# A three-layer block on one core: six tiles change places in SBUF

## The chip, the cores and the metric

The kernel runs on one core of one Trainium2 chip, in one launch. The metric is the device time of one execution in microseconds (us). The kernel before took 1033.55 us as the median of three runs (1032.76, 1033.91 and 1033.55).

## The reference, cut to what matters

The input is one sequence of 256 tokens with 1024 features, in fp32. It goes through two layers of a first block and then one layer of a second block:

```
for i in range(2):                                    # first block
    h = rmsnorm(x, norm1_g[i])
    mix = hybrid_mixer(h, w_in[i], ...)               # three kinds of attention, 16 heads of 64
    x = x + mix @ w_out[i]
    h = rmsnorm(x, norm2_g[i])
    a, u = split(h @ w_up[i], 2)                      # 2 x 2816 columns
    x = x + (silu(causal_conv(a) + conv_b[i]) * u) @ w_down[i]
h = rmsnorm(x, final_g)
u = rms_norm(h, norm_mix_pre)                         # second block
proj = u @ w_in                                       # ten slots of 256, and gates 4 x 1024
ys = [rg_lru, pool, hgrn2, short_conv](proj)          # four branches of 256 columns
merged = sum_k sigmoid(gate_k) * (ys[k] @ w_branch[k])
h = h + rms_norm(merged @ w_out, norm_mix_post)
hid = square(relu(rms_norm(h, norm_mlp_pre) @ w_up))  # 4096 columns
h = h + rms_norm(hid @ w_down, norm_mlp_post)
```

Nearly all of the arithmetic is in the products with the weight matrices.

## The kernel before, in words

**Weights and their split.** The weights come in pieces of 128 x 2048 fp32 (1 MB) through a ring of four buffers, the tile `raw`. A weight is used as the sum of two fp32r numbers, a high and a low part: ScalarE writes the high part `whi` (L1288), VectorE (L1744) or GpSimd (L2575) the difference `wlo`. Both have three slots. The activations are split in the same way, so a product of an activation and a weight is three matmuls: high by high, high by low, low by high.

**The activations' tiles.** `hb2` holds the normed input of a layer, 8 feature tiles with the high and the low part side by side (`hh` and `hl`). The names `gh` and `gl` hold the high and the low part of what goes into a second product: the hidden units of the feed-forward parts (written at L1421 and L2105, and at L1718 and L2540), part of the attention's output, and the branches of the second block. `mg` holds one quarter of the second block's merged sum. `mskt` holds the attention masks and an identity in bf16. `prmt` holds small parameters and an fp32 identity. `PQ` is a large working area; `E`, `rl`, `PT`, `gb`, `sm`, `sc`, `cc` and `th` are smaller ones.

**Which role each tile has on TensorE.** A matmul has a stationary operand, which a weight load brings into the array ahead of it, and a moving one, which streams through. In the up projections (L697, L702, L703) `whi` and `wlo` are stationary and `hb2` moves. In the down projections (L720 to L722, and L734 to L736), the branch products (L1211 to L1213) and part of the output products (L577, L578, L580) a 128 x 128 piece of `gh`, `gl` or `mg` is stationary and 512 columns of `whi` or `wlo` move. In the transposes (L554 of `X`, L773 of `PQ`, L926 of `E` and `XN`) the tile that is turned is stationary and the identity in `prmt` moves. In the profile's names the moving tile stands first, the stationary one second.

**Order.** The program of each engine is written out by hand, and the engines meet by semaphores alone. Feed-forward stage j has TensorE make 256 hidden units (16 matmuls with 512 columns and 16 with 256), ScalarE and VectorE evict, convolve and gate them, and TensorE take the 24 matmuls of a down projection a stage later. All loads are issued by the sync engine's queue; `mskt` is loaded once, near the start (L2658), and first read by L1860.

**Where tiles lie.** No address is written in the kernel. Each `sb(...)` call asks for the next piece of every SBUF partition, in the order in which the calls stand (L162 to L186). The built program begins this list at byte 16512 of a partition and rounds each start up to a multiple of 32 bytes.

Of the kernel before, what the change touches and what calls it, by code (L numbers as in the profile page):

```python
# [8 lines left out]
F32R = mybir.dt.float32r  # L9
BF16 = mybir.dt.bfloat16  # L10
# [5 lines left out]
L = 256  # L16
# [128 lines left out]
def program(nc, wst, prm, msk, prm2, gains, lvl, x, out):  # L145
    ctx = ExitStack()
    with ctx:
        def sb(name, shape, dt=F32):
            return ctx.enter_context(nc.sbuf_tensor(name, shape, dt))
# [12 lines left out]
        wlo = sb("wlo", [128, SPL, CH], F32R)  # L162
        X = sb("X", [128, 2, D])
        XN = sb("XN", [128, 2, D])
        mskt = sb("mskt", [128, 9, 128], BF16)
        hb2 = sb("hb2", [128, 8, 2, L], F32R)
        hh, hl = hb2[:, :, 0, :], hb2[:, :, 1, :]
        gh = sb("gh", [128, 2, 2, L], F32R)
        gl = sb("gl", [128, 2, 2, L], F32R)
        mg = sb("mg", [128, 2, 2, L], F32R)  # L170
        prmt = sb("prmt", [128, NPRM])
        PQ = sb("PQ", [128, 2 * PCOLS + 22 * L])
        P = PQ[:, 0:2 * PCOLS].rearrange("p (t c) -> p t c", t=2)
        QT = PQ[:, 2 * PCOLS:].rearrange("p (j q) -> p j q", q=L)
        gb = sb("gb", [128, D])
# [4 lines left out]
        sc = sb("sc", [128, 2, L])  # L180
        selm = sb("selm", [128, 2, L], BF16)
        vbd = sb("vbd", [80, 5, 64])
        cc = sb("cc", [128, 2, L])
        th = sb("th", [128, 2, L])
        lv = sb("lv", [128, 8, 128], mybir.dt.uint16)
# [6 lines left out]
        def par2(name):  # L192
            a, w = at2[name]
            return PQ[:, a:a + w]

# [14 lines left out]
        def space(n):  # L210
            a = spare["pq"]
            spare["pq"] += n
            assert spare["pq"] <= 2 * PCOLS + 22 * L
            return PQ[:, a:a + n]

# [2415 lines left out]
        def sync_program(e):  # L2631
# [24 lines left out]
            for m in range(2, NT):  # L2656
# [4 lines left out]
                if m == second:  # L2661
                    q.wait_ge(*x_new[("out", 1), 1, 1])
                    e.dma_start(PQ[:, 0:NPRM2], prm2).then_inc(s_prm2, 16)
                    e.dma_start(lv[:, :, :], lvl).then_inc(s_lvl, 16)
# [186 lines left out]
```

## Time and profile before

| | |
|---|---|
| median of three runs | 1033.55 us |
| the profiled execution's own time | 1032.76 us |
| its span, first to last instruction | 1031.5 us |
| TensorE matmuls busy | 1021.1 us, 99% of the span, 5714 matmuls |
| TensorE weight loads busy | 857.8 us, 83% |
| VectorE busy | 765.6 us, 74% |
| ScalarE busy | 551.6 us, 53% |
| GpSimd busy | 224.8 us, 22% |
| DMA | 179.16 MB, 174 GB/s over the span |

"Busy" of TensorE is the time in which at least one matmul is under way. Matmuls overlap: one with 512 columns has a duration of about 0.39 us, while the next one starts 0.23 us after it. What sets the pace of a row of matmuls is therefore the distance between starts, not the duration. A weight load stands in a row of its own (PEld), and it runs beside the matmul before it.

### The profile page before, as it was taken

The numbers are of one execution on the slowest core, as the hardware profiler recorded it, in microseconds if no ns is written. First come the engines' busy times: TensorE is split into PE (matmuls) and PEld (weight loads), VectorE is DVE, ScalarE is ACT, GpSimd is POOL, SyncE is SP. The second block draws the span as 40 slices with busy tenths as digits, with TensorE's granted clock in tenths as the row PEclk, the third lists the DMA queues.
The fourth block names the chain that finished last, engine by engine and source line by source line (L and its number), as shares of the span: only waits on it lengthen the run. The fifth ranks groups of instructions, "written<-read, shape, count | busy, mean of one in ns | idle before, by whom it ended". The sixth has DMA issues, their size and how long they took to land.

```text
span 1031.5 us, 14779 instructions
## 1 busy us (share of the span) xinstructions
PE 1021.1 (99%) x5714; PEld 857.8 (83%) x5714; DVE 765.6 (74%) x1221; ACT 551.6 (53%) x831; POOL 224.8 (22%) x311
## 2 busy tenths in 40 slices
PE   8999999999999999999999999999999999999997
PEld 6877788888888877788888888998888878888886
DVE  6987678788777887578787778978855457666665
ACT  6575656555456466656455556755434545434432
POOL 0270600000000280600000003128967620000000
PEclk9999999999999999999999999999999999999999
DMA  9451445555554351365554554543535555455541
GB/s 361 151 203 44 149 178 186 187 191 202 194 184 176 112 213 42 123 223 191 204 204 167 200 186 163 175 172 105 180 124 194 214 184 221 177 207 191 178 149 41
DMA packets 26822, 179.16 MB, mean 174 GB/s; under 512 B 2944, under 2 KB 3072, under 8 KB 6272
## 3 DMA queue, kind: packets, MB, share of 16 engines
q1 hardware_dynamic: 26752, 178.22, 48.6%
q8 instruction: 45, 0.74, 0.3%
q14 instruction: 25, 0.20, 0.1%
HBM read 177.16 MB, written 1.05 MB: 173 GB/s over the span
## 4 chain that ended last, share of the span: by engine, by line
PE 98%; DMA 1%; DVE 1%; ACT 0%; SPq 0%; issue 0%; DVEq 0%
PE pb L697 17%; PE pb L702 10%; PE pb L577 9%; PE pb L578 9%; PE pb L580 8%; PE pb L720 6%; PE pb L722 6%; PE pb L721 6%; PE pb L703 2%; PE pb L958 2%; PE pb L914 2%; PE pb L623 1%; PE pb L622 1%; PE pb L624 1%; PE pb L1124 1%; PE pb L926 1%
## 5 line engine op out<-in xcount | busy, mean ns | idle before, releaser
L1744 DVE TENSOR_TENSOR wlo<-raw,whi 128x2048 fp32r<-128x2048 f32 x127 | 290.6, 2290 | 108.3 <-ACT whi L1288 108.0
L1288 ACT ACTIVATE whi<-raw 128x2048 fp32r<-128x2048 f32 (+1 forms) x164 | 304.9, 1863 | 62.9 <-PE pb L580 31.4
L2575 POOL TENSOR_TENSOR wlo<-raw,whi 128x256 fp32r<-128x256 f32 x260 | 197.6, 798 | 322.8 <-ACT whi L1288 322.6
L697 PE MATMUL pb<-hb,whi 128*128 128x512 f32 x770 | 194.0, 391 | 0.0
L697 PEld LDWEIGHTS pb<-hb,whi 128*128 128x128 f32 x770 | 144.9, 188 | 28.8
L577 PE MATMUL pb<-whi,hb 128*128 128x512 f32 x344 | 137.9, 401 | 0.0
L578 PE MATMUL pb<-wlo,hb 128*128 128x512 f32 x344 | 134.1, 390 | 0.0
L580 PE MATMUL pb<-whi,hb 128*128 128x512 f32 x328 | 128.0, 390 | 0.0
L702 PEld LDWEIGHTS pb<-hb,wlo 128*128 128x128 f32 x880 | 120.0, 190 | 8.6
L702 PE MATMUL pb<-hb,wlo 128*128 128x256 f32 x880 | 122.7, 282 | 0.0
L720 PE MATMUL pb<-whi,gh 128*128 128x512 f32 x280 | 109.3, 391 | 0.0
L722 PE MATMUL pb<-whi,gl 128*128 128x512 f32 x280 | 109.1, 390 | 0.0
L721 PE MATMUL pb<-wlo,gh 128*128 128x512 f32 x280 | 108.9, 389 | 0.0
L2584 POOL TENSOR_TENSOR sm<-sm 128x1 f32<-128x1 f32 x12 | 6.5, 553 | 422.7 <-DVE sm L1752 242.5
L577 PEld LDWEIGHTS pb<-whi,hb 128*128 128x128 f32 x344 | 64.6, 188 | 17.8 <-issue 5.0
L578 PEld LDWEIGHTS pb<-wlo,hb 128*128 128x128 f32 x344 | 64.6, 188 | 12.5
L580 PEld LDWEIGHTS pb<-whi,hb 128*128 128x128 f32 x328 | 61.6, 188 | 13.3
L722 PEld LDWEIGHTS pb<-whi,gl 128*128 128x128 f32 x280 | 52.6, 188 | 11.4
L721 PEld LDWEIGHTS pb<-wlo,gh 128*128 128x128 f32 x280 | 52.6, 188 | 11.1
L720 PEld LDWEIGHTS pb<-whi,gh 128*128 128x128 f32 x280 | 52.7, 188 | 9.6
L1421 ACT ACTIVATE gh<-th 128x512 fp32r<-128x512 f32 x22 | 13.9, 632 | 76.3 <-DVE th L2102 76.3
L703 PE MATMUL pb<-hb,whi 128*128 128x512 f32 x110 | 43.6, 396 | 0.0
(388 smaller groups left out, 1559.2 us busy)
## 6 DMA issues: line engine op xcount, KB each, us to landing
raw<-wst SPq DMA_DIRECT2D x160, 1024.0 KB, 4.8
raw<-wst SPq DMA_DIRECT2D x8, 512.0 KB, 3.6
gb<-gains SPq DMA_DIRECT2D x3, 512.0 KB, 5.6
X<-x SPq DMA_DIRECT2D x2, 512.0 KB, 5.5
out<-X SPq DMA_DIRECT2D x4, 256.0 KB, 2.1
PQ<-prm SPq DMA_DIRECT2D x1, 909.0 KB, 4.7
raw<-wst SPq DMA_DIRECT2D x2, 256.0 KB, 7.5
prmt<-prm SPq DMA_DIRECT2D x1, 479.0 KB, 10.2
```

What stands on the lines that cost most here:

```text
L577: e.matmul(o, high[:, s], wh[:, k, :], start=first and k == 0, stop=False)
L578: mm = e.matmul(o, high[:, s], wl[:, k, :], start=False, stop=False)
L580: mm = e.matmul(o, low[:, s], wh[:, k, :], start=False, stop=last and k == 3)
L697: e.matmul(both, wh[:, k, s], hb2[:, k, :, :].rearrange("p i q -> p (i q)"), start=k == 0, stop=False)
L702: e.matmul(high, wl[:, k, s], hh[:, k, :], start=False, stop=False)
L703: mm = e.matmul(both, wh[:, 7, s], hb2[:, 7, :, :].rearrange("p i q -> p (i q)"), start=False, stop=True)
L720: e.matmul(o, ah, wh[:, k, c], start=j == 0 and k == 0, stop=False)
L721: e.matmul(o, ah, wl[:, k, c], start=False, stop=False)
L722: mm = e.matmul(o, al, wh[:, k, c], start=False, stop=last and k == 1)
L1288: e.activation(whi[:, split_slot(m), 0:w], raw[:, m % RAW, 0:w], ACT.Copy).then_inc(*hi(m))
L1744: e.tensor_tensor(wlo[:, split_slot(m), 0:w], raw[:, m % RAW, 0:w], whi[:, split_slot(m), 0:w].bitcast(F32), ALU.subtract).then_inc(*lo_v(m))
L2575: g = e.tensor_tensor(wlo[:, split_slot(m), s], raw[:, m % RAW, s], whi[:, split_slot(m), s].bitcast(F32), ALU.subtract)
```

## The change

The order of the `sb(...)` calls is changed. No shape, type, instruction, semaphore or loop is touched, and each engine has the same instructions in the same order.

```
         XN = sb("XN", [128, 2, D])
-        mskt = sb("mskt", [128, 9, 128], BF16)
         hb2 = sb("hb2", [128, 8, 2, L], F32R)
         hh, hl = hb2[:, :, 0, :], hb2[:, :, 1, :]
-        gh = sb("gh", [128, 2, 2, L], F32R)
-        gl = sb("gl", [128, 2, 2, L], F32R)
-        mg = sb("mg", [128, 2, 2, L], F32R)
         prmt = sb("prmt", [128, NPRM])
+        mskt = sb("mskt", [128, 9, 128], BF16)
         PQ = sb("PQ", [128, 2 * PCOLS + 22 * L])
...
         vbd = sb("vbd", [80, 5, 64])
+        gh = sb("gh", [128, 2, 2, L], F32R)
+        gl = sb("gl", [128, 2, 2, L], F32R)
+        mg = sb("mg", [128, 2, 2, L], F32R)
         cc = sb("cc", [128, 2, L])
```

What this does to the first byte of each tile within a partition, in the two built programs:

| tile | bytes | start before | start after | moved by | start modulo 64, before and after |
|---|---|---|---|---|---|
| raw, whi, wlo, X, XN | 98304 together | 16512 (raw) | 16512 | 0 | 0, 0 |
| mskt | 2304 | 114816 | 135584 | +20768 | 0, **32** |
| hb2 | 16384 | 117120 | 114816 | -2304 | 0, 0 |
| gh | 4096 | 133504 | 210848 | +77344 | 0, **32** |
| gl | 4096 | 137600 | 214944 | +77344 | 0, **32** |
| mg | 4096 | 141696 | 219040 | +77344 | 0, **32** |
| prmt | 4376 | 145792 | 131200 | -14592 | 0, 0 |
| PQ | 43520 | 150176 | 137888 | -12288 | 32, 32 |
| gb, rl, E, PT, sm, sc, selm, vbd | 29440 together | 193696 (gb) | 181408 | -12288 each | 32, 32 |
| cc, th, lv | 6144 together | 223136 (cc) | 223136 | 0 | 32, 32 |

## Rows read from the trace of the kernel before

**Rows 1.** The page: span, TensorE's busy time, granted clock in 40 slices.
```profile
span 1031.5 us, 14779 instructions
...
PE 1021.1 (99%) x5714; PEld 857.8 (83%) x5714; DVE 765.6 (74%) x1221; ACT 551.6 (53%) x831; POOL 224.8 (22%) x311
...
PEclk9999999999999999999999999999999999999999
```

**Rows 2.** The page: engines' shares of the chain that ended last.
```profile
PE 98%; DMA 1%; DVE 1%; ACT 0%; SPq 0%; issue 0%; DVEq 0%
```

**Rows 3.** Waits of TensorE, longest first: total us, times, longest us.
```profile
PE pb L599 <- ACT whi L1350: 1.8, 1, 1.8
PE pb L541 <- DVE sm L2556: 1.5, 1, 1.5
PE pb L681 <- DVE hb L1766: 0.8, 1, 0.8
```

**Rows 4.** Instructions grouped by line and shape: busy us, mean ns, idle before.
```profile
L720 PE MATMUL pb<-whi,gh 128*128 128x512 f32 x280 | 109.3, 391 | 0.0
...
L577 PE MATMUL pb<-whi,gh 128*128 128x512 f32 x40 | 16.6, 415 | 0.0
...
L1211 PE MATMUL pb<-whi,gh 128*128 128x512 f32 x32 | 13.2, 413 | 0.0
...
L734 PE MATMUL pb<-whi,gh 128*128 128x512 f32 x24 | 9.5, 397 | 0.0
...
L577 PE MATMUL pb<-whi,mg 128*128 128x512 f32 x8 | 3.1, 389 | 0.0
```

**Rows 5.** Timeline of TensorE in a down projection: start us, length us.
```profile
162.18 0.39 PE L722 MATMUL pb<-whi,gl 128*128 128x512 f32 x1
162.41 0.39 PE L720 MATMUL pb<-whi,gh 128*128 128x512 f32 x1
162.63 0.39 PE L721 MATMUL pb<-wlo,gh 128*128 128x512 f32 x1
```

**Rows 6.** Timeline of TensorE in an up projection.
```profile
148.51 1.75 PE L697 MATMUL pb<-hb,whi 128*128 128x512 f32 x7
150.10 1.11 PE L702 MATMUL pb<-hb,wlo 128*128 128x256 f32 x8
151.05 0.40 PE L703 MATMUL pb<-hb,whi 128*128 128x512 f32 x1
151.29 1.77 PE L697 MATMUL pb<-hb,whi 128*128 128x512 f32 x7
152.90 1.12 PE L702 MATMUL pb<-hb,wlo 128*128 128x256 f32 x8
```

**Rows 7.** Weight loads by line: ns min/median/max, first and last start.
```profile
L697 PEld LDWEIGHTS pb<-hb,whi x770: 187/188/192, 148.3 to 1013.4; 128*128 128x128 f32 x193
...
L554 PEld LDWEIGHTS pb<-prmt,X x96: 138/140/143, 4.8 to 848.3; 128*128 128x128 f32 x96
...
L773 PEld LDWEIGHTS pb<-prmt,PQ x84: 97/140/146, 26.3 to 409.3; 128*128 128x128 f32 x76, 128*32 128x32 f32 x4, 128*64 128x64 f32 x4
...
L1124 PEld LDWEIGHTS pb<-PQ,rl x32: 187/188/193, 699.4 to 752.2; 128*128 128x128 f32 x32
```

**Rows 8.** Writers of gh and gl (timeline), and a like group on other tiles.
```profile
154.64 0.63 ACT L1421 ACTIVATE gh<-th 128x512 fp32r<-128x512 f32 x1 [2.15 <-DVE th L2102]
...
155.30 0.69 DVE L2105 TENSOR_TENSOR gl<-th,gh 128x512 fp32r<-128x512 f32 x1 [0.70 <-ACT gh L1421]
...
L2083 DVE TENSOR_TENSOR E<-E,rl 128x512 f32<-128x512 f32 x22 | 15.2, 693 | 0.7
```

**Rows 9.** DMA issues (KB, median us to landing), and mskt's first reader.
```profile
gb<-gains SPq DMA_DIRECT2D x3, 512.0 KB, 5.6
...
mskt<-msk SPq DMA_DIRECT2D x1, 288.0 KB, 14.3
...
L1860 DVE TENSOR_TENSOR sc<-sc,mskt x4: 291/292/294, 40.4 to 360.4; 128x128 f32<-128x128 f32 x4
```

## The prediction

> **What bounds the kernel now.** I read the page first: TensorE has a matmul under way in 1021.1 of 1031.5 us, and the granted clock is at its upper level of 2.4 GHz in all forty slices [rows 1]. The chain that ended last is TensorE for 98% [rows 2]. The waits of TensorE come next: the three longest are 1.8, 1.5 and 0.8 us, each met once, and the longest two stand at the very start [rows 3]. So no other engine and no transfer is late anywhere for long; the kernel lasts as long as its row of 5714 matmuls, and the reader should ask of any edit whether it changes the distance between the starts of two matmuls. I read that distance from the timeline. In a down projection matmuls with 512 columns start at 162.18, 162.41 and 162.63, thus 0.225 us apart [rows 5]. In an up projection eight matmuls with 256 columns take from 150.10 to 151.05, thus 0.119 us each, and seven with 512 columns take from 148.51 to 150.10, thus 0.227 us each [rows 6].
>
> **The change part by part.** No instruction is removed, added or moved on any engine; only starts of tiles change. There are three kinds of change, and I give each a cost.
>
> First, tiles that keep their position within 64 bytes: `hb2`, `prmt`, `PQ` and the eight tiles behind it. Everything moves by a multiple of 64 bytes, and `PQ` with those behind it by one common distance, so that their mutual distances stay. The largest user is the up projection, in which `hb2` streams through the array. If the absolute place counted, the eight slices of `hb2`, which lie 2 KB apart, would stream at unlike rates. They take 1.59 us for seven in one place and 1.61 us (151.29 to 152.90) in the next [rows 6], 0.227 and 0.230 us each, over seven different slices. I take 0. The 0.02 us between the two groups, which are the same slices against other weights, is the largest irregularity of such a row. There are 110 such groups (770 matmuls of L697 by 7 [rows 7]), so 110 x 0.02 = 2.2 us is my bound for what place could give or cost here, in either direction.
>
> Second, `gh`, `gl` and `mg`, which go from 0 to 32 modulo 64 and 77344 bytes up. On TensorE they are always stationary. The matmuls that use them are five groups with counts of 280, 40, 32, 24 and 8 for the product high by high [rows 4], and each has two sisters of the same count for the other two products: 3 x 384 = 1152 matmuls. What changes for each is a weight load. Does a load from 32 modulo 64 take longer? The trace has both kinds. `X` starts at 0 modulo 64 and `PQ` at 32, and their loads have the same median of 140 ns. `whi` starts at 0 and `rl` at 32: 188 ns for both, with maxima of 192 and 193 [rows 7]. So the measured difference is 0 ns at the median. And a longer load would be covered. The fastest row of full loads is that of the 256-column matmuls, one every 0.119 us [rows 6], so a load and all that goes with it fits in 0.119 us; the matmuls on `gh` start 0.225 us apart [rows 5]. A load could grow by about 0.1 us before it showed. What hides it is the stream of the matmul before. I take 0. Without that cover, the one extra nanosecond by which the maxima differ would be 1.2 us (1152 x 1 ns), and the whole spread of a load of `rl`, 193 - 187 = 6 ns, would be 6.9 us; a gain could be as large by the same reckoning if the new place were the better one.
>
> The writers of these tiles are the other half. ScalarE writes `gh` in 0.63 us and VectorE `gl` in 0.69 us, of which the latter ends at 155.99 [rows 8]. The down projection of that stage starts at 159.66, right behind four groups of an up projection that began at 148.51 [rows 6] (eight more matmuls of each kind take 2.79 us, 148.51 + 4 x 2.79 = 159.67). So there is 3.7 us of cover for these two instructions. Their price if they changed: VectorE's operation of the same shape with all three operands on tiles at 32 modulo 64 (`E` and `rl`) takes 693 ns, against 0.69 us for the one whose output and one input are at 0 [rows 8]. I take 0 again. If the cover were gone, a change of 10 ns on each of some 40 such pairs would be 0.4 us, for better or worse.
>
> A rule bears on this half. The Trainium skill, page "Vector Engine (DVE) Microarchitecture Reference", section 5.2, says that VectorE streams at full rate only if its runs of words start on an 8-byte boundary, and gives 1.30 against 1.054 ns per column where both sources start on an odd word. Were the new starts odd words, its estimate for 512 columns would be 126 ns more per operation; at a start that is a multiple of 32 the rule sees no change, and the equal 0.69 us of the two kinds of rows [rows 8] agrees.
>
> Third, `mskt`, which also goes to 32 modulo 64. Its transfer of 288 KB lands 14.3 us after its issue, that is at about 20 us, and its first reader starts at 40.4 us [rows 9], so 20 us of cover. Transfers into a tile at 32 modulo 64 are in the trace too (`gb`, 512 KB in 5.6 us), so a multiple of the time is not to be feared; `mskt` waits in a queue of weight transfers, and even if it took twice its share (288 KB at 512 KB in 5.6 us is 3.2 us) nothing on the path would wait for it but the weights behind it. I take 0, with 0 to 3.2 us as bounds if the weights behind it were awaited by TensorE, and as much the other way.
>
> Sum: 0 us on the profiled execution, whose own time is 1032.76 us (1031.5 us of span and 1.3 us around it). That run was the fastest of the three shown; their median is 0.79 us above it. Unchanged work should land at the median, so I predict 1033.5 us.
>
> **The rivals.**
>
> *Slower: the loads of `gh`, `gl` and `mg` become visible.* The mechanism would be a load that has to fetch more from a start at 32 modulo 64, or collides with ScalarE and VectorE, which write `cc` and `th` right behind it in SBUF, and does so in a part that the stream before doesn't cover. With 6 ns on 1152 matmuls it gives 1033.5 + 6.9 = 1040.4 us; it leaves the band of no change from 1.8 ns each on (2.07 / 1152). For it speaks only that the three tiles are the ones whose position within 64 bytes changes, and that they are used 1152 times. Against it speak the equal medians [rows 7] and the room of 0.1 us.
>
> *Faster: the present place costs something.* A matmul with 512 columns would stream in 0.213 us at 2.4 GHz, and starts are 0.225 to 0.227 apart. If a part of those 12 to 14 ns were a collision due to the place of `gh` next to `hb2`, the move could give it back: 4 ns on 1152 matmuls is 4.6 us, thus 1028.9 us. Against it: the up projection, which doesn't touch `gh`, has the same 0.227 [rows 6], so the surplus belongs to every matmul.
>
> A rule speaks against both. The Trainium skill, page "SBUF — State Buffer", section "Who interferes with whom", gives TensorE two read ports of its own, for the moving operand and for the load, and names the port pair of VectorE and GpSimd as the only place of contention; no address enters it. By it alone the change is worth 0. The rows of one pace on all tiles agree, so it strengthens the forecast's chance and changes no number.
>
> *Nothing on TensorE, but the start is disturbed.* If the load of `mskt` held the weights behind it back while TensorE is nearly dry, up to 3.2 us would be added: 1036.7 us. Against it: after 0.8 us at most TensorE waits for nothing there [rows 3].
>
> That the change doesn't do what it says can be left out: the starts in the two built programs are those of the table.
>
> **How the numbers follow.** The forecast of no effect gets 0.88, the slower rival 0.05, the disturbed start 0.02, the faster rival 0.05. What a measurement of this kernel can tell from no change is about 0.2%, 2.07 us, so the band is 1031.5 to 1035.6 us. The chances are then 0.05 for faster, 0.88 for the same and 0.07 for slower. The range holds the forecast's own bounds: below, 2.2 us of irregularity (1031.3); above, the like 2.2 us and a little of the loads (1035.8). The rivals lie outside it with 0.12.
>
> **What would show each step right or wrong.** Right: starts in the down projections still 0.225 to 0.227 us apart, loads of `gh` at 188 ns, L1421 at 0.63 and L2105 at 0.69 us, seven `hb2` matmuls in 1.59 to 1.61 us, the same three waits of TensorE, and the landing of `mskt` far ahead of 40 us. A wider distance at L720 to L722 with L697 unchanged would show the slower rival; a narrower one the faster; later first weights the third. I am wrong if the time leaves 1031.5 to 1035.6 us with the granted clock unchanged.

## The result and the profile after

The changed kernel takes 1039.61 us as the median of four runs (1039.45 to 1042.50), against 1033.73 us for the kernel before beside it: a ratio of 1.0061 with a 95% interval of 1.0046 to 1.0077. It is slower by about 6 us, and outside the range that I gave. Executions of one kernel can differ by some 3 us, and by the traces most of that lies ahead of the first product on `gh` (which starts at 106.0 us in the kernel before and as late as 109.2 us in others), so a median of few runs can lie up to 3 us too high, and the lowest times stand beside the medians below.

The page and the waits of TensorE look as before, with a longer span:

```profile
span 1038.1 us, 14777 instructions
...
PE 1027.8 (99%) x5712; PEld 858.0 (83%) x5714; DVE 766.0 (74%) x1221; ACT 551.6 (53%) x831; POOL 224.5 (22%) x311
...
PEclk9999999999999999999999999999999999999999
...
PE 98%; DMA 1%; DVE 1%; ACT 0%; issue 0%; SPq 0%; DVEq 0%
```

The busy time of TensorE has grown by 6.7 us (1021.1 to 1027.8), the span by 6.6 us [rows 1]; the granted clock is the same. No engine waits in a new place. TensorE's waits after the change (total us, times, longest) are those of [rows 3], to a tenth:

```profile
PE pb L599 <- ACT whi L1350: 1.8, 1, 1.8
PE pb L541 <- DVE sm L2556: 1.5, 1, 1.5
PE pb L681 <- DVE hb L1766: 0.8, 1, 0.8
```

So the matmuls themselves have become slower, and the groups by line and shape tell which (busy us, mean ns of one):

```profile
L697 PE MATMUL pb<-hb,whi 128*128 128x512 f32 x770 | 194.7, 392 | 0.0
L577 PE MATMUL pb<-whi,hb 128*128 128x512 f32 x344 | 137.9, 401 | 0.0
...
L702 PE MATMUL pb<-hb,wlo 128*128 128x256 f32 x880 | 122.7, 282 | 0.0
L722 PE MATMUL pb<-whi,gl 128*128 128x512 f32 x280 | 110.9, 396 | 0.0
L720 PE MATMUL pb<-whi,gh 128*128 128x512 f32 x280 | 110.6, 395 | 0.0
L721 PE MATMUL pb<-wlo,gh 128*128 128x512 f32 x280 | 110.5, 395 | 0.0
...
L577 PE MATMUL pb<-whi,mg 128*128 128x512 f32 x8 | 3.2, 396 | 0.0
```

Before, L720 had 391 ns and L577 with `mg` 389 ns [rows 4]; L721 and L722, which I had not shown, had 389 and 390 ns. The products on `hb2` are unchanged (L577) or nearly so (L697, 0.7 us more over 770). Each product with `gh`, `gl` or `mg` stationary is longer on average, by 4 to 7 ns in most groups and by 2 to 3 ns in the 120 of L577, L578 and L580 on `gh` and `gl`.

The pace is in the timeline. One down projection after the change, its first matmuls and the first of what follows (start us, length us):

```profile
159.88 0.39 PE L720 MATMUL pb<-whi,gh 128*128 128x512 f32 x1
160.11 0.40 PE L721 MATMUL pb<-wlo,gh 128*128 128x512 f32 x1
160.35 0.39 PE L722 MATMUL pb<-whi,gl 128*128 128x512 f32 x1
...
162.21 0.40 PE L721 MATMUL pb<-wlo,gh 128*128 128x512 f32 x1
162.44 0.40 PE L722 MATMUL pb<-whi,gl 128*128 128x512 f32 x1
162.67 0.40 PE L720 MATMUL pb<-whi,gh 128*128 128x512 f32 x1
162.91 0.40 PE L721 MATMUL pb<-wlo,gh 128*128 128x512 f32 x1
...
165.47 0.85 PE L697 MATMUL pb<-hb,whi 128*128 128x512 f32 x3
```

The same stretch in the kernel before:

```profile
159.66 0.39 PE L720 MATMUL pb<-whi,gh 128*128 128x512 f32 x1
...
165.13 1.07 PE L697 MATMUL pb<-hb,whi 128*128 128x512 f32 x4
```

24 matmuls take 5.59 us instead of 5.47, 0.233 us each instead of 0.228. (The 0.225 us that the prediction read from [rows 5] came from three rounded starts.) That is 5 ns per matmul, and from the starts of all of them I count 4.6 us over the 840 of L720 to L722; the other 312 with these tiles give 1.4 us more, and the 770 matmuls of L697 0.7 us. Together this is 6.7 us, which accounts for the 6.6 us of the span.

The loads of these tiles, on which I had built my argument, show nothing at all. After the change (ns min/median/max):

```profile
L720 PEld LDWEIGHTS pb<-whi,gh x280: 186/188/192, 159.7 to 1026.1; 128*128 128x128 f32 x140
...
L722 PEld LDWEIGHTS pb<-whi,gl x280: 187/188/188, 160.1 to 1026.6; 128*128 128x128 f32 x140
```

### The profile page after: what moved, and what is told of

Same layout as the page of the kernel before. It is cut to its first block, busy times and chain, and to the rows that moved or that the text cites. A ratio compares the mean times of both kernels' runs of the same rounds, so it can differ in the third digit from the quotient of the medians.

```text
span 1038.1 us, 14777 instructions
## 1 busy us (share of the span) xinstructions
PE 1027.8 (99%) x5712; PEld 858.0 (83%) x5714; DVE 766.0 (74%) x1221; ACT 551.6 (53%) x831; POOL 224.5 (22%) x311
## 4 chain that ended last, share of the span: by engine, by line
PE 98%; DMA 1%; DVE 1%; ACT 0%; issue 0%; SPq 0%; DVEq 0%
PE pb L697 17%; PE pb L702 10%; PE pb L577 9%; PE pb L578 9%; PE pb L580 8%; PE pb L722 6%; PE pb L721 6%; PE pb L720 6%; PE pb L703 2%; PE pb L958 2%; PE pb L914 2%; PE pb L623 1%; PE pb L624 1%; PE pb L622 1%; PE pb L1124 1%; PE pb L926 1%
## 5 line engine op out<-in xcount | busy, mean ns | idle before, releaser
L697 PE MATMUL pb<-hb,whi 128*128 128x512 f32 x770 | 194.7, 392 | 0.0
L697 PEld LDWEIGHTS pb<-hb,whi 128*128 128x128 f32 x770 | 144.9, 188 | 29.8
L577 PE MATMUL pb<-whi,hb 128*128 128x512 f32 x344 | 137.9, 401 | 0.0
L578 PE MATMUL pb<-wlo,hb 128*128 128x512 f32 x344 | 134.1, 390 | 0.0
L580 PE MATMUL pb<-whi,hb 128*128 128x512 f32 x328 | 128.1, 391 | 0.0
L702 PEld LDWEIGHTS pb<-hb,wlo 128*128 128x128 f32 x880 | 120.1, 190 | 8.7
L702 PE MATMUL pb<-hb,wlo 128*128 128x256 f32 x880 | 122.7, 282 | 0.0
L722 PE MATMUL pb<-whi,gl 128*128 128x512 f32 x280 | 110.9, 396 | 0.0
L720 PE MATMUL pb<-whi,gh 128*128 128x512 f32 x280 | 110.6, 395 | 0.0
L721 PE MATMUL pb<-wlo,gh 128*128 128x512 f32 x280 | 110.5, 395 | 0.0
L577 PEld LDWEIGHTS pb<-whi,hb 128*128 128x128 f32 x344 | 64.6, 188 | 17.9 <-issue 5.0
L578 PEld LDWEIGHTS pb<-wlo,hb 128*128 128x128 f32 x344 | 64.7, 188 | 12.7
L580 PEld LDWEIGHTS pb<-whi,hb 128*128 128x128 f32 x328 | 61.6, 188 | 13.2
L722 PEld LDWEIGHTS pb<-whi,gl 128*128 128x128 f32 x280 | 52.6, 188 | 12.6
L721 PEld LDWEIGHTS pb<-wlo,gh 128*128 128x128 f32 x280 | 52.6, 188 | 12.5
L720 PEld LDWEIGHTS pb<-whi,gh 128*128 128x128 f32 x280 | 52.7, 188 | 11.0
L1421 ACT ACTIVATE gh<-th 128x512 fp32r<-128x512 f32 x22 | 13.9, 632 | 76.3 <-DVE th L2102 76.3
```

Source lines behind the costliest of these rows:

```text
L577: e.matmul(o, high[:, s], wh[:, k, :], start=first and k == 0, stop=False)
L578: mm = e.matmul(o, high[:, s], wl[:, k, :], start=False, stop=False)
L580: mm = e.matmul(o, low[:, s], wh[:, k, :], start=False, stop=last and k == 3)
L697: e.matmul(both, wh[:, k, s], hb2[:, k, :, :].rearrange("p i q -> p (i q)"), start=k == 0, stop=False)
L702: e.matmul(high, wl[:, k, s], hh[:, k, :], start=False, stop=False)
L720: e.matmul(o, ah, wh[:, k, c], start=j == 0 and k == 0, stop=False)
```

## The experiments

Every experiment changes only where tiles lie. `gap` and `gap2` are tiles that nobody uses. Where room was needed, the tile `sm` was cut from 1152 to as few as 1120 columns, which suffice. Since the starts themselves turned out not to be what counts, the table gives differences of starts modulo 256, which is where the series ended; the texts on record speak of 64 and 128, as I thought at the time. The ratio is near that of the means of all executions, not of the medians, and is taken against the kernel before beside each run (whose medians there were 1033.0 to 1033.7 us). The last column is read from the traces: how much longer than in the kernel before the part of the span is that begins with the first product on `gh`. It leaves out the early stretch in which executions of one kernel differ.

| kernel | gh minus whi | hb2 minus whi | median us (lowest) | ratio to before, 95% interval | behind the first use of gh, us |
|---|---|---|---|---|---|
| before | 0 | 0 | 1033.73 (1032.76) | | |
| after | 32 | 0 | 1039.61 (1039.45) | 1.0061 (1.0046 to 1.0077) | +6.5 |
| high place, 64 | 64 | 0 | 1042.32 (1040.32) | 1.0072 (1.0057 to 1.0087) | +6.4 |
| old place, 32 | 32 | 0 | 1043.09 (1040.41) | 1.0072 (1.0054 to 1.0090) | +7.6 |
| hb2 shifted | 64 | 32 | 1045.91 (1045.80) | 1.0110 (1.0093 to 1.0127) | +11.6 |
| weights shifted | 32 | 32 | 1045.04 (1044.89) | 1.0103 (1.0085 to 1.0120) | +10.8 |
| high place, 0 | 0 | 0 | 1033.20 (1032.70) | 1.0005 (0.9992 to 1.0017) | 0.0 |
| all shifted by 32 | 0 | 0 | 1032.77 (1032.62) | 0.9989 (0.9980 to 0.9999) | -0.1 |
| all at multiples of 512 | 0 | 0 | 1035.24 (1032.82) | 1.0010 (1.0000 to 1.0021) | +0.1 |
| gh at 16 | 16 | 0 | 1041.71 (1040.09) | 1.0072 (1.0054 to 1.0089) | +6.3 |
| after, weights follow | 0 | 0 | 1033.47 (1032.81) | 1.0001 (0.9989 to 1.0012) | -0.1 |
| gh at 128 | 128 | 0 | 1039.42 (1039.26) | 1.0052 (1.0034 to 1.0070) | +6.3 |
| gl alone at 32 | 0 (gl: 32) | 0 | 1042.06 (1039.12) | 1.0070 (1.0051 to 1.0089) | +6.1 |
| low parts shifted | 0 (wlo differs) | 0 | 1039.67 (1037.42) | 1.0049 (1.0034 to 1.0064) | +3.9 |
| gh at 192 | 192 | 0 | 1038.23 (1035.87) | 1.0038 (1.0026 to 1.0051) | +2.9 |
| gh at 4 | 4 | 0 | 1039.52 (1039.35) | 1.0061 (1.0044 to 1.0078) | +6.5 |

Differences to `wlo` are the same as to `whi` except in the kernel with the low parts shifted, since the two lie 24576 bytes, 96 x 256, apart. The pieces of these tiles that a matmul takes begin at multiples of 512 bytes within them, so the differences hold for every piece. With `hb2` or the weights shifted, products ahead of the first use of `gh` are slower too, and are not in the last column.

### Place or position?

The changed kernel, `gh` at the end of SBUF but back at 0 modulo 64:

```
         vbd = sb("vbd", [80, 5, 64])
+        sb("gap", [128, 8])
         gh = sb("gh", [128, 2, 2, L], F32R)
```

> The changed kernel with 32 unused bytes ahead of gh: gh, gl and mg stay at the end of SBUF (210880 and on) but start at 0 modulo 64 again (64 modulo 128); cc, th and lv move by 32 bytes too. In the changed kernel the 512-column matmuls that have gh, gl or mg stationary start 0.231 to 0.235 us apart instead of 0.227. Theory 1, the start modulo 64 of the stationary tile costs: 0.227 again, 1033.5 to 1034.0 us. Theory 2, the place at the end of SBUF, beside cc and th, costs: 0.233 as in the changed kernel, 1039.5 us. Theory 3, it is the start modulo 128 that counts: 1039.5 us too, and then the next kernels tell 2 from 3.

The kernel before, `gh`, `gl` and `mg` 32 bytes on:

```
+        sb("gap", [128, 8])
         gh = sb("gh", [128, 2, 2, L], F32R)
         gl = sb("gl", [128, 2, 2, L], F32R)
         mg = sb("mg", [128, 2, 2, L], F32R)
+        sb("gap2", [128, 8])
```

> The kernel before with 32 unused bytes ahead of gh and 32 behind mg: gh, gl and mg stay in their old place but start at 32 modulo 64; prmt and all behind it move by 64 and keep their position modulo 64. Theory 1 (start modulo 64 of the stationary tile): 1152 matmuls x 5.7 ns = 6.6 us more than before, 1039.5 to 1040.5 us, starts 0.233 us apart in the down projections, loads still 188 ns. Theory 2 (place): as before, 1033.7 us. Theory 3 (modulo 128; gh goes from 0 to 32): 1039.5 to 1040.5 us.

Both are slow, the first at 1040.3 and the second at 1040.4 us at their lowest. The second shows that the old place gives no protection: 32 bytes in it cost all of the 6 us, so theory 2 alone can't be the explanation. The first disproves theory 1: a start at 0 modulo 64 does not bring the time back. Theory 3 passes both.

### The role of each tile

```
+        sb("gap", [128, 8])
         hb2 = sb("hb2", [128, 8, 2, L], F32R)
+        sb("gap2", [128, 8])
```

> The kernel before with 32 unused bytes ahead of hb2 and 32 behind it: only hb2 is at 32 modulo 64 (gh, gl, mg and prmt go to 0 modulo 64 and 64 modulo 128). hb2 is the stationary tile of 1056 matmuls with 512 columns and the moving one of 960 with 512 and 1392 with 256 columns. Theory 1, with a price for the stationary role alone: 1056 x 5.7 ns = 6.0 us, 1039.7 us, distances at L577, L578, L580 near 0.233 us and at L697, L702 as before. If a moving tile pays as well: 960 x 5.7 = 5.5 us more at the least, 1045 us or above. Theory 2 (place): 1033.7 us. Theory 3 (modulo 128): like theory 1 plus 6.6 us for gh, gl and mg, 1046 us.

```
+        sb("gap", [128, 8])
         whi = sb("whi", [128, SPL, CH], F32R)
         wlo = sb("wlo", [128, SPL, CH], F32R)
+        sb("gap2", [128, 8])
```

> The kernel before with 32 unused bytes ahead of whi and 32 behind wlo: only whi and wlo are at 32 modulo 64. They are stationary in 960 matmuls with 512 and 1392 with 256 columns, and moving in 2208 with 512. Theory 1, stationary role alone: 960 x 5.7 = 5.5 us, and for the 256-column ones, whose starts are 0.119 us apart so that less covers a load, between 0 and more than 5.7 ns each (7.9 us): 1039 to 1047 us or above. If the moving role pays too: 2208 x 5.7 = 12.6 us on top, 1052 us or above. Theory 2 (place): 1033.7 us.

Both came out some 12 us above before (1045.9 and 1045.0 us), and their groups are alike. Those of the kernel with `hb2` shifted:

```profile
L699 PE MATMUL pb<-hb,whi 128*128 128x512 f32 x770 | 197.1, 395 | 0.0
L579 PE MATMUL pb<-whi,hb 128*128 128x512 f32 x344 | 139.7, 406 | 0.0
...
L704 PE MATMUL pb<-hb,wlo 128*128 128x256 f32 x880 | 120.7, 279 | 0.0
L724 PE MATMUL pb<-whi,gl 128*128 128x512 f32 x280 | 110.7, 395 | 0.0
```

(L699, L579, L704 and L724 are L697, L577, L702 and L722 of the other listings.) Now every product with 512 columns is slow: 395 against 391 ns where `hb2` moves, 406 against 401 where it is stationary. So a tile pays in either role. And the products with 256 columns are *faster*, 279 against 282 ns. That shifting `hb2` and shifting the weights do the same to the pair of the two was the hint that the pair is what counts.

### Each tile, or the difference of two?

```
-        sm = sb("sm", [128, 1152])
+        sm = sb("sm", [128, 1120])
...
+        sb("gap", [128, 24])
         gh = sb("gh", [128, 2, 2, L], F32R)
```

> The changed kernel with 96 unused bytes ahead of gh (and 128 unused bytes of sm given up to make room): gh, gl and mg lie at the end of SBUF, at 210816 and on, and start at 0 modulo 128. Theory 3 (a start off a multiple of 128 costs, wherever the tile lies): 0.227 us between starts in the down projections, 1033.6 us. Theory 2 (the place at the end of SBUF): 0.233 us, 1039.5 us or above.

```
+        sb("gap", [128, 8])
         raw = sb("raw", [128, RAW, CH])
```

> The kernel before with 32 unused bytes ahead of everything: raw, whi, wlo, X, XN, mskt, hb2, gh, gl, mg and prmt all start at 32 modulo 128, PQ and what follows at 64. Stationary and moving tile of every large matmul thus have the same start modulo 128, but not 0. Theory 3a, each tile must start at a multiple of 128: all 512-column distances 0.233, 256-column ones 0.1165 to 0.117, about 1045.5 us, as with the two kernels in which only hb2, or only whi and wlo, were at 32. Theory 3b, only the difference of the two starts counts (two reads of one memory that get in each other's way): 0.227 and 0.120 as before, 1033.6 us.

The first measured 1033.20 us, with the three tiles at the very end of SBUF, so the place is innocent. The second measured 1032.77 us with every tile at 32 modulo 128. Its groups are those of before:

```profile
L698 PE MATMUL pb<-hb,whi 128*128 128x512 f32 x770 | 194.0, 391 | 0.0
...
L703 PE MATMUL pb<-hb,wlo 128*128 128x256 f32 x880 | 122.7, 282 | 0.0
L721 PE MATMUL pb<-whi,gh 128*128 128x512 f32 x280 | 109.3, 391 | 0.0
```

Theory 3a falls and 3b stands. I then put it to the changed kernel itself: `gh`, `gl` and `mg` stay at the very bytes at which they are slow, and the weights and `hb2` go to 32 as well.

```
+        sb("gap", [128, 8])
         raw = sb("raw", [128, RAW, CH])
...
-        sm = sb("sm", [128, 1152])
+        sm = sb("sm", [128, 1144])
```

> The changed kernel with gh, gl and mg at exactly its own bytes (210848, 214944, 219040: 32 modulo 128), and 32 unused bytes ahead of raw, so that whi, wlo and hb2 are at 32 modulo 128 as well (32 bytes of sm given up for it). If the difference of the two starts modulo 128 is what counts: 0.227 us again in the down projections, 1033.0 us. If gh at 32 is slow of itself: 0.233, 1039.5 us.

1033.47 us, a ratio of 1.0001. Its trace has L721, the product of `gh` and `whi`, at 391 ns as in the kernel before. All 6 us are back with `gh`, `gl` and `mg` still at the bytes at which they were slow. This is the run on which I rest the explanation.

### How the difference counts

```
+        prmt = sb("prmt", [128, NPRM])
+        sb("gap", [128, 24])
         raw = sb("raw", [128, RAW, CH])
...
-        mskt = sb("mskt", [128, 9, 128], BF16)
...
-        prmt = sb("prmt", [128, NPRM])
...
         lv = sb("lv", [128, 8, 128], mybir.dt.uint16)
+        mskt = sb("mskt", [128, 9, 128], BF16)
```

> The kernel before in another order of tiles: prmt first, mskt last, 96 unused bytes, so that raw, whi, wlo, X, XN, hb2, gh, gl, mg, PQ and nearly all others start at a multiple of 512 (before: of 128 at most, and PQ and what follows at 32 modulo 128). Theory 3 with 128 as the whole rule: the large matmuls as before, 0.227; PQ, E, rl and the others feed matmuls of fp32 with 0.109 us between starts whether at 0 or 32, so nothing there: 1033.0 to 1033.7 us. Theory 4, larger multiples than 128 give more: distances of 512-column matmuls under 0.225, below 1031 us.

Nothing gained: the product of L720 takes 390 ns (391 before) and that of L697 391, and the lowest time is 1032.82 us. The median, 1035.24 us, is higher, but the span behind the first use of `gh` differs by 0.1 us only. Larger multiples don't help.

```
-        gh = sb("gh", [128, 2, 2, L], F32R)
-        gl = sb("gl", [128, 2, 2, L], F32R)
-        mg = sb("mg", [128, 2, 2, L], F32R)
+        gx = sb("gx", [128, 3080], F32R)
+        gh, gl, mg = (gx[:, 1024 * i + 4:1024 * i + 1028].rearrange(...) for i in range(3))
+        sb("gap", [128, 8])
```

> The kernel before with gh, gl and mg cut from one tile of 3080 columns at an offset of 16 bytes: they start at 16 modulo 128; prmt goes to 64 modulo 128. Starts at 32 and at 64 cost the same 6 ns per matmul. If any start off 128 pays in full: 0.233 us, 1040 to 1041 us. If the price grows with the offset or begins at 32: 0.227 to 0.230 us, 1033.6 to 1037 us.

The next two have a `gap` of 32 and of 48 columns ahead of `gh`, the third is the kernel with `gx` cut at an offset of one column instead of four.

> The kernel before with 128 unused bytes ahead of gh (sm shorter by 128): gh, gl and mg start at 0 modulo 256 while whi, wlo and hb2 are at 128 modulo 256. If the differences count modulo 128: 0.227, 1033.0 us. If modulo 256: 0.233, 1039.5 us. In all kernels so far the fast pairs had a difference of 0 modulo 256, so this is open.

> The kernel before with 192 unused bytes ahead of gh (sm shorter by 128): gh, gl and mg differ from whi, wlo and hb2 by 192 modulo 256. Differences of 16, 32, 64 and 128 all cost 5 to 6 ns per matmul. If every difference but 0 modulo 256 pays: 0.232 to 0.234 us between starts in the down projections, 1038.5 to 1040 us. If the price falls towards 256 or only the lower half pays: 0.227 to 0.230 us, 1033 to 1036 us.

> The kernel before with gh, gl and mg cut from one tile at an offset of one column, 4 bytes. If a difference of any size pays in full: 0.232 to 0.234 us, 1039 to 1041 us. If blocks of 16 bytes or more are what is compared: 0.227 us, 1033 us.

Differences of 4, 16, 32, 64 and 128 bytes all cost about the same: 5.9 to 7.6 us between the lowest times of each and of the kernel before beside it, and 6.3 to 7.6 us in the last column. (Why the old place at 32 has the 7.6, 1.1 us more than any other of these, no run shows.) 128 is slow, so the rule is modulo 256 and not 128; and before the change `hb2` and `gh` were 256 away from `whi` modulo 512 (117120 and 133504 against 49280), so that 256 itself is harmless. 192 costs less: 2.4 us at the lowest time (1035.87 against 1033.47), 4.7 us at the medians and 2.9 us in the last column. Its groups are uneven, 394 ns for the product of `gh` and `whi`, 393 for `gl` and `whi` and 389, as before, for `gh` and `wlo`, although all three pairs differ by 192. So the price is not the same on both sides of a multiple of 256, the remainder alone doesn't set it, and my two alternatives for this run were both too simple.

### Which load and which stream?

```
         gh = sb("gh", [128, 2, 2, L], F32R)
+        sb("gap", [128, 8])
         gl = sb("gl", [128, 2, 2, L], F32R)
+        sb("gap2", [128, 24])
```

> The kernel before with gl alone moved by 32 bytes (gh, mg, hb2, whi, wlo stay at 0 modulo 128). A down projection runs gh on whi, gh on wlo, gl on whi, in turn. 384 of the 1152 matmuls have gl stationary. If the price belongs to the pair of a load and the stream that runs meanwhile, or to the pair of one matmul, and is additive: 384 x 5.7 = 2.2 us, 1035.2 us, and only one of three distances in the down projection is long; which of them tells whether it is the load (the distance before L722) or the matmul's own stream (behind L722). If one unequal tile disturbs the whole row: up to 6.6 us.

The groups of this kernel (L722, L723, L724 are L720, L721, L722 of the others):

```profile
L723 PE MATMUL pb<-wlo,gh 128*128 128x512 f32 x280 | 111.5, 398 | 0.0
L722 PE MATMUL pb<-whi,gh 128*128 128x512 f32 x280 | 110.7, 395 | 0.0
L724 PE MATMUL pb<-whi,gl 128*128 128x512 f32 x280 | 109.2, 390 | 0.0
```

The matmul that has `gl` stationary, and so the unequal pair of its own, is *not* the slow one: 390 ns as before. The slow one is the matmul ahead of it, `gh` on `wlo`, with 398 ns. The timelines of matmuls and loads suggest why. Matmuls, then loads, of the same stretch:

```profile
161.68 0.40 PE L723 MATMUL pb<-wlo,gh 128*128 128x512 f32 x1
161.92 0.39 PE L724 MATMUL pb<-whi,gl 128*128 128x512 f32 x1
```

```profile
161.45 0.19 PEld L723 LDWEIGHTS pb<-wlo,gh 128*128 128x128 f32 x1
161.68 0.19 PEld L724 LDWEIGHTS pb<-whi,gl 128*128 128x128 f32 x1
```

The load of `gl` for L724 starts at 161.68, at the moment at which the stream of `wlo` for L723 starts. So the run speaks for the load and the stream that run at the same time as the two that interfere, and it is the stream that becomes longer, while the load keeps its 188 ns. My expectation of additivity failed: 384 loads of 1152 have an unequal start, but the lowest time is 1039.12 us, the full price. Of the two streams that have only equal companions, one is slow as well: `gh` on `whi` (L722), two matmuls after the disturbed one, with 395 ns, while the one between, L724, is not. How a disturbance gets there, no run shows. The starts in the trace say the same: behind L722, L723 and L724 the next matmul starts 232, 237 and 229 ns later (228, 227 and 228 before).

### A version meant to be faster

Since 256-column products gained 3 ns where 512-column ones lost 5, I shifted only the low part of the weights, and only in the tiles in which it is stationary for 256 columns.

```
+        def low_slot(m):
+            n = split_slot(m)
+            a = (0, CH + 32, 2 * CH + 32)[n] + ((8, -8, 8)[n] if plan[m][0] == "f" else 0)
+            return wlo[:, a:a + CH]
```

> A version meant to be faster. Where hb2 and the weights had unlike starts, 512-column matmuls took 6 ns more but 256-column ones 3 ns less (0.1165 to 0.117 against 0.120). The low part of the weights is stationary in 256-column matmuls in the feature-wise tiles (up projections and the second block's input), and moving in 512-column ones elsewhere. Here the low part of feature-wise tiles alone is written 32 bytes off within its slot, all else stays at 0 modulo 128 (wlo moved behind mg, slots 8320 bytes apart). If the gain belongs to the 256-column pairs: 1104 x 3.3 = 3.6 us less, 1029.5 us, with at most some 200 transitions of 6 ns back (1.2 us): 1029.5 to 1030.7 us. If it appears only where the 512-column matmuls around are slow too: 1033.0 us.

It took 1039.67 us. The experiment was built on the wrong modulus: the slots keep their position modulo 128, but the second and third lie at 128 modulo 256 relative to `whi`, and so pay in the other products (394 ns for `gh` on `wlo` in place of 389). The group of 256-column products (L702 before) takes 122.4 us in place of 122.7, where shifting `hb2` had given 120.7. Why so little is left of the gain the run can't tell: the shifted low parts lie at 32, 96 or 160 modulo 256 by their slot, and the 512-column products of the same rows are nearly as fast as before (392 ns). One detail bears on the last section. The last 512-column stream of `hb2` ahead of a 256-column one has an equal pair of its own, and beside it the first shifted low part is loaded; by the starts in the traces (121 such) it is 234 ns ahead of its successor in place of 227. I have no version that beats the kernel before.

## Why the prediction was wrong

**What bounds the kernel** held: TensorE's row of matmuls, its waits and the clock are unchanged, and the distance between starts is what moved.

**First kind of tile** (those that keep their position): right in substance. The large groups on other tiles kept their duration; L697 grew by 0.7 us, inside the bound of 2.2 us.

**Third kind** (`mskt`): right. It lands 14.3 us after its issue as before.

**Second kind**: the writers were as predicted (L1421 632 ns, L2105 693 ns). The loads failed. "I take 0" for 1152 matmuls measured 6.0 us directly and 0.7 us in the rows behind them. Three links of that step broke.

- *I asked the wrong question.* I compared loads by the position of one tile modulo 64. What counts is the difference between two tiles modulo 256. Two kernels with the same `gh` address are 6 us apart, depending on where the weights lie.
- *The trace of before held no sample.* All its 512-column products on split operands had a difference of 0 modulo 256. My samples of loads from 32 modulo 64, in [rows 7], were of other types and shapes. `rl` was loaded beside streams of 256 fp32 columns: that of `PQ` begins 34920 bytes into the tile and is 152 off modulo 256, that of `gb` is equal, and the trace of before has both, at medians of 377 and 379 ns. `PQ` was loaded beside the identity in `prmt`, for most of its pieces 32 off modulo 256, but in transposes of 128 columns, which show no loss. A cost that the nearest rows can't show has to be called unknown; I called it measured.
- *The cover argument was about the wrong thing.* "A load could grow by about 0.1 us before it showed" assumed that interference would lengthen the load. The load has 188 ns in the slow kernels too; its companion, the stream, is longer, and nothing covers the stream, because it is the path. On a path made of one engine's pace, a loss of 5 ns can't be hidden.

The rows of `rl` in the kernel before, of an unequal and of an equal pair (ns min/median/max):

```profile
L1124 PE MATMUL pb<-PQ,rl x32: 377/377/383, 699.6 to 752.4; 128*128 128x256 f32 x32
...
L1124 PE MATMUL pb<-gb,rl x24: 377/379/382, 706.8 to 742.5; 128*128 128x256 f32 x24
```

The rival "slower" had the right tiles, count and size (6 ns on 1152 gives 1040.4 us, 1039.6 measured), but the wrong mechanism: neither a start at 32 as such nor `cc` and `th` close by is to blame, since the high place at 0 is fast, and the changed kernel's own bytes are fast once the weights follow. I gave it 0.05, for the equal medians of the loads, the cover, and a rule. The Trainium skill, page "SBUF — State Buffer", section "Who interferes with whom", has the two reads of TensorE on ports of their own that wait for no one. The runs don't agree with that as a statement on time: the load of one matmul and the stream of another cost 6 us between them, by their addresses alone (that it is these two, rather than the matmul's own pair, rests on the kernel with `gl` alone moved). The measurement decides. I had let a rule strengthen the forecast's chance at a step for which there was no row of the same pair and shape.

## What to carry to other kernels

Where TensorE's pace is the bound and its operands are fp32r with 512 columns, lay the stationary and the moving tiles, and the pieces taken from them, at starts that are equal modulo 256 bytes, and check this after any change of sizes or order of allocations; a reordering that moves no instruction can cost 0.5 to 1.1%, as measured in this one kernel; bf16 operands were not tried. When pricing a change of layout, look for a row with the same pair and the same shape, not for one with the same tile; if there is none, the cost is unknown and the range must say so.

## What the runs showed of the hardware

- A 512-column fp32r matmul and the weight load beside it go at 0.227 to 0.230 us per matmul if the two tiles' starts differ by a multiple of 256 bytes, and at 0.232 to 0.234 us for differences of 4 to 128 bytes. At 192 the loss is smaller and uneven: 394, 389 and 393 ns for the three products of a down projection (391, 389 and 390 before).
- The duration of the load (188 ns) doesn't show it; that of the matmul does (389 to 391 against 395 ns).
- 256-column fp32r products behave the other way: 282 ns if equal, 279 ns if all tiles of the row are unequal. Those in fp32 (L1124) hardly tell: 379 ns if equal, 377 ns at 152. Transposes with 128 columns don't care: before the change `X` and the identity were equal modulo 256 (47360 bytes apart) and `PQ` and the identity, for most pieces, were not (4384 bytes), and the matmuls of L554 and L773 have the same median of 272 ns.
- Alignment as such is worth nothing here: all tiles at 32 modulo 128 give 1032.62 us at the lowest, all at multiples of 512 give 1032.82 us.
